# A token-mixing layer on one core: two q and k pairs as plain products, then q, k, xp and four gate tiles as six units of seven block products

## The chip, the cores and the metric

One NeuronCore of one Trainium2 chip. The metric is the device time of one execution in microseconds (us), the median of 3 runs for the kernel before. The profile and the trace are of one further execution of the same program, with a span and a time of its own.

## The reference

```python
# SEQ 1024, D_MODEL 1024, D_FF 2816, POOL_WIDTH 512, 8 heads of 64; depth 1, batch 1, float32
h = x + 0.5 * swiglu(rmsnorm(h, ffn1_norm), ffn1_w_gate_up, ffn1_w_down)
u = rmsnorm(h, mix_norm)
proj = u @ w_in                        # columns: xp 512 | q 512 | k 512 | v 512 | gate logits 2048
y_pool = causal_pool_mixer(xp, pool_w_group, pool_scale) @ w_branch_pool
# four groups of 128 channels: mean over a trailing window of 2, 4, 8, 16 minus the token, then a 128x128 map, a scale
o_sb = stick_breaking_attention(q, k, v)
# per head: z = q.k / 8; A[t,s] = sigmoid(z[t,s]) * prod_{s<j<t} (1 - sigmoid(z[t,j])), s < t; o = A @ v
y_sb = o_sb @ w_branch_attn
g_pool, g_sb = split(sigmoid(gate_logits))
h = h + (g_pool * y_pool + g_sb * y_sb) @ w_out
h = h + 0.5 * swiglu(rmsnorm(h, ffn2_norm), ffn2_w_gate_up, ffn2_w_down)
out = rmsnorm(h, final_norm)
```

## The kernel before

The whole layer is one program with the instructions of each engine written out in their order. TensorE (PE) multiplies, ScalarE (ACT) and VectorE (DVE) prepare operands and take results, GpSimd (POOL) does small work, and SyncE (SP) issues nearly all transfers in one order. Engines meet only through semaphores, and an instruction that waits holds back everything behind it on its engine.

**Products.** Every float32 operand is split in a high part, which ACT copies with rounding (`w_hi`, `u_hi`), and a low part, the rest, which DVE subtracts (`w_lo`, `u_lo`). One product of 128 x 128 by 128 x 512 is then three: high by high, high by low and low by high. One tile of an output projection (128 columns of w_in by 512 tokens, one of PSUM's eight banks) sums over 8 blocks of 128 rows of D_MODEL, so it costs 24 such products. The feed-forward parts and the pool branch save products with a scheme of seven block products in place of eight (`PRODUCTS`: which bank, which sum of weights, and which block or sum of the other side); the projections by w_in are plain.

**Stages.** First feed-forward part 0 to 661.9 us, the front of the mixing block to 883, attention to 1166.5, the attention branch and the out projection to about 1300, second feed-forward part to the end.

**Front** (line 1192 on). `unit_quad` makes two tiles for all tokens in four banks, 96 products, from one unit of weights (`w_raw`, 1 MB, two slots). The order on PE is: two quads for xp, the pooling map of half the groups (`group_quad`, 12 products), values in eight tiles of 24 products in two halves of D_MODEL with the second `group_quad` in between, four units of the pool branch (`pool_branch_unit`, seven products of 6 each), four quads for q and k. Under them ACT copies xp to `xpad`, DVE adds shifted copies of it for the windows (L2327 is a form of it), DVE splits each unit's weights (L1905), q and k are split and stored in `qk_dram`, and the pool branch's result goes to `g_dram`.

**Attention** (line 1383 on). 8 heads of 8 row tiles (`TILE_ORDER` 7, 6, 1, 0, 5, 4, 3, 2; a tile qt has (qt + 1) x 128 columns) give 64 steps and 4 to drain. Each tile goes through a chain over three steps: PE makes the logits (L1334, L1336; in step s); ACT takes the sigmoids `keep` and `a`; GpSimd sets the diagonal to zero (L2626); DVE scans `keep` into the running product (L2471) and multiplies it into `a` (L2475); PE transposes `a` (L1349; in step s + 2); ACT and DVE split what it turned (`at_hi` L1826, `at_lo` L2484); after every second tile PE weighs the values with it (`weigh`, L1365, L1366). The gates' products (L1188) are spread between these as filler: eight units of 96, 768 in all, one unit being gate tile j of the pool branch and gate tile j of the attention branch. `SHARE` says how much of it each step gets, by the row tile:

```python
SHARE = {7: 8, 6: 16, 1: 16, 0: 11, 5: 4, 4: 12, 3: 13, 2: 12}
cut = g0 + (g1 - g0) // 2
gate_parts(g0, cut)
if s >= 4 and s % 2 == 0: weigh((s - 4) // 2)
if 2 <= s < NA + 2: turn(s - 2)
```

Behind the turn come the tile's one or two logits, with the other half of the step's filler after each of them in equal parts. Under attention DVE also splits the gate weights by pieces (L2496), GpSimd multiplies the finished pool gates into y_pool (L2633), and SP loads q and k of a head (L865) two heads ahead; those of heads 0 and 1 are loaded before attention, once the pool branch's result is stored.

## Time and profile before

| | |
|---|---|
| median of 3 runs | 1938.36 us (1938.32 to 1938.59) |
| span of the profiled execution | 1937.1 us |
| that execution's own time | 1938.4 us |
| instructions | 25171 |
| PE busy | 1923.7 us, 99% |
| DVE busy | 1338.3 us, 69% |
| ACT busy | 772.0 us, 40% |
| GpSimd busy | 136.9 us, 7% |
| DMA | 347.20 MB, mean 179 GB/s |

Busy time of PE counts modelled ends of pipelined matmuls, so 99% is not the share in which PE works at its peak. Times in a trace are from the span's start; durations of a group are means.

### The profile page before, as it was taken

The numbers are of one execution on the slowest core, as the hardware profiler recorded it, in microseconds if no ns is written. First come the engines' busy times: TensorE is split into PE (matmuls) and PEld (weight loads), VectorE is DVE, ScalarE is ACT, GpSimd is POOL, SyncE is SP. The second block draws the span as 40 slices with busy tenths as digits, with TensorE's granted clock in tenths as the row PEclk, the third lists the DMA queues.
The fourth block names the chain that finished last, engine by engine and source line by source line (L and its number), as shares of the span: only waits on it lengthen the run. The fifth ranks groups of instructions, "written<-read, shape, count | busy, mean of one in ns | idle before, by whom it ended". The sixth has DMA issues, their size and how long they took to land.

```text
span 1937.1 us, 25171 instructions
## 1 busy us (share of the span) xinstructions
PE 1923.7 (99%) x9094; PEld 1607.4 (83%) x9094; DVE 1338.3 (69%) x1656; ACT 772.0 (40%) x1154; POOL 136.9 (7%) x218
## 2 busy tenths in 40 slices
PE   9999999999999999999999999999999999999998
PEld 9888888888888888888888888888888888888887
DVE  6987777775566667425777778789767776755655
ACT  7423232333434424214565652464323232324344
POOL 1000000000000100002333320010000000000002
PEclk9999999999999999999999999999999999999999
DMA  5456645468676503546645347643535454677665
GB/s 163 148 202 229 226 160 164 171 219 309 201 237 194 179 24 103 177 152 190 164 131 161 108 148 249 206 143 109 183 132 187 149 184 139 221 262 241 206 192 204
DMA packets 245092, 347.20 MB, mean 179 GB/s; under 512 B 16144, under 2 KB 150032, under 8 KB 240400
## 3 DMA queue, kind: packets, MB, share of 16 engines
q1 hardware_dynamic: 245008, 346.09, 54.9%
q8 instruction: 51, 0.84, 0.2%
q14 instruction: 33, 0.27, 0.0%
HBM read 232.79 MB, written 112.98 MB: 178 GB/s over the span
## 4 chain that ended last, share of the span: by engine, by line
PE 55%; DVE 2%; DMA 1%; issue 1%; ACT 1%; SPq 0%; POOL 0%; POOLq 0%; DVEq 0%; ACTq 0%
PE bank L1091 20%; PE bank L1188 12%; PE bank L1135 4%; PE bank L1137 4%; PE bank L1136 4%; PE bank L1047 2%; PE bank L1257 2%; PE bank L1285 2%; PE bank L1349 2%; DMA dn_lo_raw<-act_dram 1%; PE bank L1366 1%; PE bank L1365 1%; PE bank L1336 1%; PE bank L1334 1%; DVE tail_p L2471 0%
## 5 line engine op out<-in xcount | busy, mean ns | idle before, releaser
L1905 DVE TENSOR_TENSOR dn_lo<-dn_lo_raw,dn_hi 128x1024 fp32r<-128x1024 f32 x149 | 181.8, 1224 | 151.6 <-ACT dn_hi L1545 151.2
L1091 PE MATMUL bank<-hi_t,wa_hi 128*128 128x512 f32 x640 | 249.1, 389 | 0.2 <-issue 0.2
L1091 PE MATMUL bank<-hi_t,wa_lo 128*128 128x512 f32 x640 | 249.0, 389 | 0.0
L1091 PE MATMUL bank<-lo_t,wa_hi 128*128 128x512 f32 x640 | 249.0, 389 | 0.0
L1545 ACT ACTIVATE dn_hi<-dn_lo_raw 128x1024 fp32r<-128x1024 f32 x149 | 158.0, 1061 | 217.6 <-DMA dn_lo_raw<-act_dram 217.6
L1135 PE MATMUL bank<-dn_hi 128*128 128x512 f32 x596 | 232.7, 390 | 0.6 <-DVE dn_lo L1905 0.6
L1136 PE MATMUL bank<-dn_hi,dn_lo 128*128 128x512 f32 x596 | 231.9, 389 | 0.0
L1137 PE MATMUL bank<-dn_lo,dn_hi 128*128 128x512 f32 x596 | 231.9, 389 | 0.0
L1091 PE MATMUL bank<-hi_b,wa_hi 128*128 128x512 f32 x480 | 186.9, 389 | 0.5 <-DVE up L2029 0.5
L1091 PE MATMUL bank<-lo_b,wa_hi 128*128 128x512 f32 x480 | 186.8, 389 | 0.0
L1091 PE MATMUL bank<-hi_b,wa_lo 128*128 128x512 f32 x480 | 186.7, 389 | 0.0
L1905 DVE TENSOR_TENSOR wa_lo<-wa_lo_raw,wa_hi 128x1024 fp32r<-128x1024 f32 x132 | 174.3, 1350 | 5.6 <-ACT wa_hi L1485 0.5
L1188 PE MATMUL bank<-u_hi,w_hi 128*128 128x512 f32 x448 | 175.5, 392 | 0.0
L1188 PE MATMUL bank<-u_hi,w_lo 128*128 128x512 f32 x448 | 175.2, 391 | 0.0
L1188 PE MATMUL bank<-u_lo,w_hi 128*128 128x512 f32 x448 | 175.1, 391 | 0.0
L1525 ACT ACTIVATE g<-g 128x512 f32<-128x512 f32 x80 | 50.1, 627 | 263.9 <-DVE g L2037 257.7
L1091 PEld LDWEIGHTS bank<-hi_t,wa_hi 128*128 128x128 f32 x640 | 120.1, 188 | 25.4 <-issue 0.6
L1091 PEld LDWEIGHTS bank<-hi_t,wa_lo 128*128 128x128 f32 x640 | 120.1, 188 | 25.1
L1091 PEld LDWEIGHTS bank<-lo_t,wa_hi 128*128 128x128 f32 x640 | 120.1, 188 | 24.9
L1135 PEld LDWEIGHTS bank<-dn_hi 128*128 128x128 f32 x596 | 111.9, 188 | 24.6 <-DVE dn_lo L1905 1.7
L1137 PEld LDWEIGHTS bank<-dn_lo,dn_hi 128*128 128x128 f32 x596 | 111.9, 188 | 23.3
L1136 PEld LDWEIGHTS bank<-dn_hi,dn_lo 128*128 128x128 f32 x596 | 111.9, 188 | 23.2
(237 smaller groups left out, 3555.3 us busy)
## 6 DMA issues: line engine op xcount, KB each, us to landing
wa_lo_raw<-in_ffn_w_gate_up_dram SPq DMA_DIRECT2D x87, 512.0 KB, 5.0
dn_lo_raw<-act_dram SPq DMA_DIRECT2D x149, 256.0 KB, 4.3
act_dram<-g SPq DMA_DIRECT2D x44, 512.0 KB, 4.5
wd_t<-in_ffn_w_down_dram SPq DMA_DIRECT2D x44, 512.0 KB, 6.6
act_dram<-s_of SPq DMA_DIRECT2D x88, 256.0 KB, 6.5
wd_dram<-wd_t SPq DMA_DIRECT2D x22, 1024.0 KB, 6.0
dn_lo_raw<-wd_dram SPq DMA_DIRECT2D x85, 256.0 KB, 3.3
dn_lo_raw<-in_ffn_w_down_dram SPq DMA_DIRECT2D x64, 256.0 KB, 3.0
```

The source lines that it names most:

```text
L1047: last = nc.tensor.matmul(dst[:, cols], lhs, rhs, start=n == 0, stop=n == 3 * KT - 1, skip_group_check=True)
L1091: last = nc.tensor.matmul(acc, lhs, rhs, start=n == 0 and i != 2 and i < 5, stop=n == 11, skip_group_check=True)
L1135: nc.tensor.matmul(dst, a_hi_[:, toks], w_hi_, start=kf == 0 and DOWN[i][2], stop=False, skip_group_check=True)
L1136: nc.tensor.matmul(dst, a_lo_[:, toks], w_hi_, start=False, stop=False, skip_group_check=True)
L1137: end = nc.tensor.matmul(dst, a_hi_[:, toks], w_lo_, start=False, stop=last, skip_group_check=True)
L1188: last = nc.tensor.matmul(dst, lhs, (rhs_lo if p == 1 else rhs_hi)(kt), start=m == 0, stop=m == 3 * KT - 1)
L1257: last = nc.tensor.matmul(bank[:, b, :], weights(w_lo if p == 2 else w_hi, kt), (rhs_lo if p == 1 else rhs_hi)(kt), start=n == 0, stop=n = ...
L1285: last = nc.tensor.matmul(bank[:, 4 * s + place, :], pool_block(w_lo if p == 2 else w_hi, par, slot)[:, kt, :], rhs, start=n == 0 and i != ...
L1349: last = nc.tensor.transpose(bank[:, 5 + tb % 2, (kb % 4) * P:(kb % 4 + 1) * P], weights_of(n)[:, kb * P:(kb + 1) * P], ident[:, :])
L1525: nc.scalar.activation(g[s][:, half, :], g[s][:, half, :], ACT.Silu).then_inc(silu_ok, 1)
L1545: nc.scalar.activation(hi, raw, ACT.Copy).then_inc(dn_hi_ok, 1)
L1905: return nc.vector.tensor_tensor(dst, raw, hi.bitcast(f32), ALU.subtract)
```

## The change

The matmuls of six projections in the front go to a new unit, `mix_unit`, and two of the eight gate units leave attention.

- q and k of pairs 2 and 3 (heads 0 to 3 in order of time) come first, as two plain quads (`U_A`), right after the first feed-forward part.
- Then six block units (`MIX_UNITS`): q and k of pair 0, of pair 1, the attention branch's gate tiles 0 and 1, then 2 and 3, and the two pairs of xp. Each computes two tiles for 1024 tokens as a 2 x 2 block product with 7 products of 12 in place of 96. ACT and DVE need for it four sums of u (`mix_raw`, `mix_sum`, `tu_*`, 128 x 2048 each; two of the first four raw sums are added by GpSimd), four sums of weights per unit (`ws_*`, 128 x 512 each), and five additions of banks (`mix_c11`, `mix_c22`, `mix_c12`, `mix_c21`). The weights come whole in `ws_raw`, which has one slot: the load of unit b + 1 waits for the last low part of unit b.
- Results of q, k and gates go through a ring of three tiles (`ring_raw`, `ring_hi`, `ring_lo`) to `qk_dram` and `g_dram`; finished gates are read back after attention as those of the other tiles are.
- xp now comes last, so the pooling sums, the pooling map and the values follow in another order: values 0 to 3 of the first half, 0 and 1 of the second, group 0, values 2 and 3, the first half of 4 to 7, group 1, the second half of 4 to 7, then the four units of the pool branch, and attention directly.
- Attention has `NG` = 6 gate units, 576 products. `SHARE` is the same for each row tile; the first step gets 16 shares more (`HEAD_SHARE`). The banks of attention are dealt out anew: gates in 4 and 5, logits in 6, 7 and 0, turned tiles in 1 and 2, outputs in 3.
- Head 0 is loaded after the fourth product of the last branch unit, once the ring's stores have landed; the second slot's load follows behind that unit. ACT's wait for the stored pool branch moves from the start of attention to its third tile.

```diff
+EARLY = 4
+GATE_UNITS = tuple(((0, j), (0, j + 1)) for j in range(0, EARLY, 2)) + tuple(((0, j), (1, j)) for j in range(EARLY, KT))
+NG = len(GATE_UNITS)
+MIX_UNITS = (tuple(("qk", pair) for pair in PAIR_ORDER[2:]) + tuple(("gate", j) for j in range(0, EARLY, 2))
+             + (("xp", 0), ("xp", 1)))
+HEAD_SHARE = 16
 ...
     shares = [SHARE[x["qt"]] for x in TILES] + [4] * DRAIN
+    shares[0] += HEAD_SHARE
     shares[1] += 8
 ...
+            def load_mix(b):
+                kind, which = MIX_UNITS[b]
+                if b:
+                    sp_.wait_ge(mb_lo, 4 * b)
 ...
             def load_head(hn):
 ...
-                    sp_.wait_ge(qk_sp[pair], 32)
+                    sp_.wait_ge(pool_prod, 6 * (KT // 2 - 1) + 4)
+                    for i in range(3):
+                        sp_.wait_ge(ring_sp[i], 32 * ring_uses(i))
 ...
+            def mix_unit(b):
+                s = (b + 1) % 2
+                for i in range(7):
+                    place, hi, lo, (kind, slot) = PRODUCTS[i]
 ...
+                    if i % 2 == 0:
+                        pe.wait_ge(mb_lo, 4 * b + i // 2 + 1)
 ...
+                    if i >= 5:
+                        pe.wait_ge(mb_add, 5 * b + i - 3)
+                    for n in range(12):
+                        kt, p = n // 3, n % 3
+                        if kind == "b":
+                            rhs = u_part(u_lo if p == 1 else u_hi, slot)[:, kt, :]
+                        else:
+                            rhs = (tu_lo if p == 1 else tu_hi)[:, slot, kt, :]
+                        last = nc.tensor.matmul(bank[:, 4 * s + place, :], ws_lo[:, lo, kt, :] if p == 2 else ws_hi[:, hi, kt, :], rhs,
+                                                start=n == 0 and i != 2 and i < 5, stop=n == 11, skip_group_check=True)
+                    last.then_inc(mb_prod, 1)
 ...
-                unit_quad(U_P[m], U_P[m] % 2, Q_P[m], fresh=m == 0)
+                unit_quad(U_A[m], U_A[m] % 2, Q_A[m], fresh=m == 0)
+            for b in range(NM):
+                mix_unit(b)
+            values(0, range(4))
+            values(1, range(2))
             group_quad(0)
-            values(0, range(NT))
-            values(1, range(4))
+            values(1, range(2, 4))
+            values(0, range(4, NT))
             group_quad(1)
             values(1, range(4, NT))
             for u in range(KT // 2):
                 pool_branch_unit(u)
-            for m in range(4):
-                unit_quad(U_QK + m, (U_QK + m) % 2, Q_QK + m)
```

On DVE a block unit is worked off in this order, with parts of the next unit's weights in between:

```diff
+            def mix_unit(b):
 ...
+                mix_c11(b)
+                if b + 1 < NM:
+                    mix_weight_sums(b + 1)
+                    mix_lo(b + 1, 0)
+                mix_out(b, 0, 0, 1)
+                mix_c22(b, 0)
+                if b + 1 < NM:
+                    mix_lo(b + 1, 1)
+                mix_c22(b, 1)
+                mix_out(b, 1, 1, 2)
+                mix_c12(b)
+                if b + 1 < NM:
+                    mix_lo(b + 1, 2)
+                mix_out(b, 0, 1, 3)
```

How the filler changes in a head shows on PE in the second head, from the last logits of row tile 4 to the weighing that stands ahead of the turn of row tile 5. Before:

```order
L1334 MATMUL bank<-k_hi_214,q_st 128x512 [waits sg_ok]
L1336 MATMUL bank<-k_lo_215,q_st 128x512
L1188 MATMUL bank<-u_hi,w_hi 128x512
L1188 MATMUL bank<-u_lo,w_hi 128x512
L1188 MATMUL bank<-u_hi,w_lo 128x512
L1188 MATMUL bank<-u_hi,w_hi 128x512
L1188 MATMUL bank<-u_lo,w_hi 128x512
L1188 MATMUL bank<-u_hi,w_lo 128x512
L1188 MATMUL bank<-u_hi,w_hi 128x512
L1188 MATMUL bank<-u_lo,w_hi 128x512
L1188 MATMUL bank<-u_hi,w_lo 128x512
L1365 MATMUL bank<-at_hi,v_w 128x256 [waits ohi,alo]
```

Of the change:

```order
L1497 MATMUL bank<-k_hi_226,q_st 128x512 [waits sg_ok]
L1499 MATMUL bank<-k_lo_227,q_st 128x512
L1308 MATMUL bank<-u_hi,w_hi 128x512
L1308 MATMUL bank<-u_lo,w_hi 128x512
L1308 MATMUL bank<-u_hi,w_lo 128x512
L1308 MATMUL bank<-u_hi,w_hi 128x512
L1308 MATMUL bank<-u_lo,w_hi 128x512
L1308 MATMUL bank<-u_hi,w_lo 128x512
L1532 MATMUL bank<-at_hi,v_w 128x256 [waits ohi,alo]
```

Nine gate products have become six; the steps around this one shrink alike, and nothing else in a head moves.

On DVE in block unit 0, from its first bank sum to the ones that the sixth product (L2598) and the seventh (L2592) need, the change has (`ws_raw` and `ws_lo` are the weights of unit 1):

```order
L2584 TENSOR_TENSOR ring_raw_208<-bank,ring_raw_208 128x512 [waits mb_prod,mb_copied]
L2567 TENSOR_TENSOR ws_raw<-ws_raw 128x512 [waits mb_in]
L2569 TENSOR_TENSOR ws_raw<-ws_raw 128x512 [waits mb_sum]
L2570 TENSOR_TENSOR ws_raw<-ws_raw 128x512
L2572 TENSOR_TENSOR ws_raw<-ws_raw 128x512 [waits mb_sum]
L2143 TENSOR_TENSOR ws_lo<-ws_raw,ws_hi 128x1024 [waits mb_hi]
L2616 SCALAR_TENSOR_TENSOR ring_lo_211<-ring_raw_208,ring_hi_214 128x512 [waits mb_post]
L2598 TENSOR_TENSOR ring_raw_209<-bank,mid 128x512 [waits mb_prod,mb_copied,ring_sp2]
L2143 TENSOR_TENSOR ws_lo<-ws_raw,ws_hi 128x1024 [waits mb_hi]
L2592 TENSOR_TENSOR ring_raw_209<-bank,ring_raw_209 128x512 [waits mb_add,mb_prod]
```

The first of the four weight sums waits for the weights of unit 1 to land (`mb_in`); the sums of unit 0's own banks, L2598 and L2592, stand behind it.

On SP, where attention's first loads stand, before:

```order
L703 DMA w_raw<-in_w_in_dram 128x8x128 [waits wlo,whi]
L704 DMA w_raw<-in_w_in_dram 128x8x128
L703 DMA w_raw<-in_w_in_dram 128x8x128 [waits wlo,whi]
L704 DMA w_raw<-in_w_in_dram 128x8x128
L816 DMA qk_dram<-qk_hi_207 128x2048 [waits acc_free2,acc_free3,acc_free1,acc_free0]
L816 DMA qk_dram<-qk_lo_209 128x2048
L865 DMA q_st<-qk_dram 64x1024 [waits y_sp3,y_odd_sp,y_sp2,qk_sp2,y_sp1,y_sp0]
L865 DMA q_st<-qk_dram 64x1024
L865 DMA k_hi_214<-qk_dram 64x1024 x2
```

Of the change:

```order
L790 DMA w_raw<-in_w_in_dram 128x8x128 [waits wlo,whi]
L791 DMA w_raw<-in_w_in_dram 128x8x128
L985 DMA q_st<-qk_dram 64x1024 [waits ring_sp1,ring_sp2,ring_sp0,pool_prod]
L985 DMA q_st<-qk_dram 64x1024
L985 DMA k_hi_226<-qk_dram 64x1024 x2
L985 DMA k_lo_227<-qk_dram 64x1024 x2
L944 DMA g_dram<-pst_odd 128x512 [waits acc_free1]
L944 DMA g_dram<-pst 128x512 [waits pool_mid]
L944 DMA g_dram<-pst 128x512 [waits acc_free2]
L944 DMA g_dram<-pst 128x512 [waits acc_free3]
L985 DMA q_st<-qk_dram 64x1024 [waits acc_ready]
```

The first head's load no longer stands behind the stores of q and k in the last quads, and has a wait on the branch's products (`pool_prod`) in place of one on all stores of the pool branch. Those of the last branch unit come behind it.

## Rows read from the trace of the kernel before

**Rows 1.** The page: each engine's busy time, share and instructions; the granted TensorE clock in 40 slices.

```profile
PE 1923.7 (99%) x9094; PEld 1607.4 (83%) x9094; DVE 1338.3 (69%) x1656; ACT 772.0 (40%) x1154; POOL 136.9 (7%) x218
...
PEclk9999999999999999999999999999999999999999
```

**Rows 2.** Timeline of PE in head 2: start us, us, engine, line, operation.

```profile
961.40 0.39 PE L1188 MATMUL bank<-u_hi,w_lo 128*128 128x512 f32 x1
...
963.66 0.40 PE L1188 MATMUL bank<-u_hi,w_hi 128*128 128x512 f32 x1
```

**Rows 3.** Windows: us; PE, PEld, DVE, ACT, POOL busy (x); PEclk, DMA share, GB/s.

```profile
953.54:986.66 33.12, 33.12 (x190) 28.68 (x189) 25.98 (x33) 20.41 (x48) 12.14 (x18) 1.00 0.60 167
707.40:756.40 49.00, 49.00 (x217) 40.42 (x216) 35.82 (x48) 21.81 (x35) 0.00 (x0) 1.00 0.16 49
883.00:1166.50 283.50, 281.26 (x1569) 240.67 (x1568) 218.01 (x264) 167.87 (x388) 97.98 (x144) 1.00 0.52 149
```

**Rows 4.** PE's groups (busy us, mean ns | idle before, releaser) and its table of waits.

```profile
L1349 PE MATMUL bank<-ident,a 128*128 128x128 f32 x288 | 43.1, 276 | 1.0 <-DVE at_lo L2484 0.6 <-DVE a L2475 0.4
...
L1365 PE MATMUL bank<-at_hi,v_w 128*128 128x256 f32 (+1 forms) x160 | 38.2, 274 | 1.2 <-DVE at_lo L2484 1.2
...
PE bank L1285 <- DVE pst L2408: 0.3, 1, 0.3
```

**Rows 5.** Timeline of DVE in one head, 953.54 to 986.66.

```profile
953.54 2.29 DVE L2471 TENSOR_TENSOR_SCAN tail_p<-keep,zero_col 128x1024 f32<-128x1024 f32 x1 [1.05 <-ACT a L1812]
...
965.23 1.16 DVE L2484 TENSOR_TENSOR at_lo<-bank,at_hi 128x512 fp32r<-128x512 f32 x2 [1.76 <-ACT at_hi L1826]
...
973.61 0.96 DVE L2475 TENSOR_TENSOR a<-a,tail_p 128x767 f32<-128x767 f32 x1
...
982.16 0.69 DVE L2475 TENSOR_TENSOR a<-a,tail_p 128x511 f32<-128x511 f32 x1
982.77 0.78 DVE L2496 TENSOR_TENSOR w_lo<-w_raw,w_hi 128x512 fp32r<-128x512 f32 x1
```

**Rows 6.** Timeline of PE in the same head.

```profile
966.49 0.34 PE L1365 MATMUL bank<-at_hi,v_w 128*128 128x256 f32 x1
...
974.87 0.84 PE L1349 MATMUL bank<-ident,a 128*128 128x128 f32 x6
...
983.35 0.62 PE L1349 MATMUL bank<-ident,a 128*128 128x128 f32 x4
```

**Rows 7.** Groups of DVE; then DMA issues: KB each, us to landing.

```profile
L1996 DVE TENSOR_TENSOR wa_lo_raw<-wa_lo_raw 128x512 f32<-128x512 f32 x40 | 27.7, 692 | 1.4
...
L2327 DVE TENSOR_TENSOR s_a<-xpad 128x1039 f32<-128x1039 f32 x4 | 5.0, 1240 | 11.3 <-ACT xpad L1700 7.4 <-issue 3.7
...
L1905 DVE TENSOR_TENSOR w_lo<-w_raw,w_hi 128x2048 fp32r<-128x2048 f32 x13 | 29.8, 2291 | 10.7 <-ACT w_hi L1658 10.7
...
w_raw<-in_w_in_dram SPq DMA_DIRECT2D x32, 512.0 KB, 5.9
...
k_lo<-qk_dram SPq DMA_DIRECT2D x16, 256.0 KB, 6.3
```

**Rows 8.** GpSimd's multiply as a group and in the timeline, with DVE's scans of 384.

```profile
L2633 POOL TENSOR_TENSOR gst<-gst,pool_y 128x512 f32<-128x512 f32 x16 | 21.3, 1333 | 19.1 <-ACT gst L1854 19.1
...
982.98 1.72 POOL L2633 TENSOR_TENSOR gst<-gst,pool_y 128x512 f32<-128x512 f32 x1
...
983.47 2.04 DVE L2471 TENSOR_TENSOR_SCAN tail_p<-keep,zero_col 128x384 f32<-128x384 f32 x1
...
1150.69 0.96 DVE L2471 TENSOR_TENSOR_SCAN tail_p<-keep,zero_col 128x384 f32<-128x384 f32 x1 [0.24 <-POOL a L2626]
```

**Rows 9.** Timeline: PE and DVE at the first branch unit, SP at the head's load.

```profile
756.56 0.39 PE L1285 MATMUL bank<-yp_hi,w_hi 128*128 128x512 f32 x1
...
759.65 0.41 DVE L2285 TENSOR_TENSOR v_st<-bank,v_st 128x256 fp32r<-128x256 f32 x1
...
871.48 1.24 SPq L865 DMA_DIRECT2D k_lo<-qk_dram  x2
```

More of the change, by code:

```diff
@@ L443, in macaron_layer @@
         ms_sum = sem("ms_sum")
-        late_in = [sem(f"late_in{i}") for i in range(3)]
         part_ok = sem("part_ok")
@@ L1681, in take_qk @@
-            def take_qk(m):
-                for b in range(4):
-                    th, ab = b // 2, b % 2
-                    if b == 0 and m >= 2:
-                        act.wait_ge(qk_sp[m - 2], 32)
-                    act.wait_ge(acc_ready, 4 * (Q_QK + m) + b + 1)
-                    c = ab * SEQ + th * HALF
-                    nc.scalar.activation(qk_hi[m % 2][:, c:c + HALF], bank[:, b, :], ACT.Copy,
-                                         scale=1.0 if ab else QSCALE).then_inc(ev_hi, 1)
@@ new lines, in mix_sums_hi, with mix_hi @@
+            def mix_sums_hi(slot, sums):
+                act.wait_ge(rt_sum, sums)
+                nc.scalar.activation(tu_hi[:, slot], tu_raw[:, slot], ACT.Copy).then_inc(rt_hi, 1)
+            def mix_hi(b, g):
+                if g in (0, 3):
+                    act.wait_ge(mb_in, 32 * (b + 1))
+                else:
+                    act.wait_ge(mb_sum, 4 * b + 2 * g)
+                mix_free(act, b, g)
+                nc.scalar.activation(ws_hi[:, mix_group_hi(g)], ws_raw[:, mix_group(g)], ACT.Copy).then_inc(mb_hi, 1)
@@ new lines, in mix_post @@
+            def mix_post(b, a, th, adds):
+                kind = MIX_UNITS[b][0]
+                if kind == "xp":
+                    return
+                act.wait_ge(mb_add, 5 * b + adds)
+                if kind == "gate":
+                    nc.scalar.activation(mix_dst(b, a, th), mix_dst(b, a, th), ACT.Sigmoid).then_inc(mb_post, 1)
+                else:
+                    nc.scalar.activation(ring_hi[tile_of(b, a) % 3][:, th * HALF:(th + 1) * HALF], mix_dst(b, a, th), ACT.Copy,
+                                         scale=1.0 if a else QSCALE).then_inc(mb_post, 1)
@@ new lines, in mix_weight_sums @@
+            def mix_weight_sums(b):
+                a11, a12, s2, s1, s3, s4, a21, a22 = (ws_raw[:, s].rearrange("p k f -> p (k f)") for s in range(8))
+                dve.wait_ge(mb_in, 32 * (b + 1))
+                nc.vector.tensor_tensor(s1, a21, a22, ALU.add).then_inc(mb_sum, 1)
+                dve.wait_ge(mb_sum, 4 * b + 1)
+                nc.vector.tensor_tensor(s2, s1, a11, ALU.subtract).then_inc(mb_sum, 1)
+                nc.vector.tensor_tensor(s3, a11, a21, ALU.subtract).then_inc(mb_sum, 1)
+                dve.wait_ge(mb_sum, 4 * b + 2)
+                nc.vector.tensor_tensor(s4, a12, s2, ALU.subtract).then_inc(mb_sum, 1)
@@ new lines, in mix_lo, with mix_c11 @@
+            def mix_lo(b, g):
+                dve.wait_ge(mb_hi, 4 * b + g + 1)
+                low(flat(ws_lo[:, mix_group(g)]), flat(ws_raw[:, mix_group(g)]), flat(ws_hi[:, mix_group_hi(g)])).then_inc(mb_lo, 1)
+            def mix_c11(b):
+                dve.wait_ge(mb_copied, 2 * b + 1)
+                dve.wait_ge(mb_prod, 7 * b + 2)
+                dst = mix_dst(b, 0, 0)
+                nc.vector.tensor_tensor(dst, bank[:, 4 * ((b + 1) % 2) + 1, :], dst, ALU.add).then_inc(mb_add, 1)
@@ L2613, in _, with mix_raw @@
             norm_rows(1)
+            def mix_raw(slot):
+                nc.gpsimd.tensor_tensor(tu_raw[:, slot], u_part(u_hi, slot).bitcast(f32), u_part(u_lo, slot).bitcast(f32), ALU.add).then_inc(ut_raw, 1)
             pool.wait_ge(dn_ok, TAKEN)
-            nc.gpsimd.memset(xpad[:, :, 0:PAD], 0.0).then_inc(const_set, 1)
+            pool.wait_ge(tr_free, 3 * NT)
+            mix_raw(1)
+            for t in (6, 7):
+                pool.wait_ge(h_sp[t], 16)
+            pool.wait_ge(xn_ok, 2 * NT)
+            mix_raw(0)
+            for m in range(2):
+                pads_free(pool, m)
+                nc.gpsimd.memset(xpad[m][:, :, 0:PAD], 0.0).then_inc(const_set, 1)
             def weights_of(n):
```

685 lines of the change are left out of this document (448 added, 237 removed).

## The prediction

> **What bounds the kernel now.** I read the page first: TensorE (PE) is busy for 99% of a span of 1937.1 us, at a granted clock of full speed, 2.4 GHz, in all 40 slices [rows 1]. The reader should see that no other engine comes near, and then distrust the 99%, since matmuls overlap in the records. The timeline gives the price that counts: one 128x512 product is recorded as 0.39 us long, but eleven of them start 2.26 us apart from first to last [rows 2], which is 0.226 us each (0.2267 over longer runs). That is the unit of every sum below. The windows by stage come next [rows 3]: the front, from the first projection to attention, 661.9 to 883 us, has a single wait of 0.3 us [rows 4]; attention, 883 to 1166.5, has 218 us of VectorE (DVE) work in 283.5. The table of PE's waits lists about 2 us for attention (L1349 and L1365), with slacks so thin that they decide this case.
>
> **Products saved.** Before, the two xp pairs and four q/k pairs cost 6 x 96 products and the eight gate pairs 768. Now two pairs stay plain (192), six units cost 7 x 12 = 84 each (504), and six gate units remain (576). 1344 become 1272: 72 fewer, 72 x 0.2267 = **16.3 us**. By place, the front gains 120 products (+27.2 us) and attention loses 192 (-43.5 us). The kernel is as long as PE if PE is never starved, so the question is what those 192 hid.
>
> **Attention.** The gate products are filler. A tile's logits go out in step s; ScalarE (ACT), GpSimd's mask, DVE's scan and multiply follow; PE turns the result in step s+2. I compare the end of the multiply with the start of the transposes over one head [rows 5, 6]: for qt 5, 974.57 against 974.87 (slack 0.3 us); for qt 3, 982.85 against 983.35 (0.5); and at_lo of qt 6 ends at 966.39 with PE's weighing at 966.49 (0.1). The other turns have about a microsecond or more. SHARE is unchanged, so each head's filler falls from 87.6 to 63.1 products, by 28%. Between logits and turn of a tile lie a quarter (half for one-chunk tiles) of its own step's filler, all of the next and half of the one after. For qt 5 that is about 1 + 11.5 + 6 products, of which 5.2 go: 1.2 us against 0.3 of slack, so PE waits 0.9. For qt 3, 6 + 11.5 + 4 lose 6: 1.4 against 0.5, wait 0.9. For the weighing after qt 6, half of steps 0 and 5 lose 2: 0.5 against 0.1, wait 0.4. The other turns lose about as much as they have, and the waits ahead of them cover the rest. Sum 2.2 us a head. A second reading agrees: from this scan of qt 7 to the next the head takes 33.1 us, and DVE is busy for 26.0 of them [rows 3, 5]. It is idle for 7.1, of which 24.5 products, 5.6 us, would go: DVE would have to be busy for 94% of the time, in short chains that each wait for ACT and PE. The first head gets extra filler (HEAD_SHARE), so 7 x 2.2 = **15.4 us** of waits. From below it could be nothing, if DVE starts earlier as PE hurries; from above some 24 us, if each of the eight turns waits for DVE's own queue.
>
> **Front: six block units.** No row shows this form here, so I take the ordinary 128x512 product [rows 2] at 0.2267; a unit is 19.0 us. DVE does per unit five bank sums and four weight sums of 128x512 (0.69 us each), three low parts of 128x1024 at 1.23 and, for q and k, four more of 0.69 [rows 7]: 12 to 13 us, which fits. The order does not fit everywhere. The next weights can be loaded only when the last low part of this unit is done, and DVE then stands before the weight sums while c22, which the sixth product needs at 5 x 2.72 = 13.6 us, is behind them. In unit 0 the last low part is at about 4 us (DVE takes the last plain bank first); 5.9 us to landing plus the spilled megabytes ahead of it [rows 7] gives 10.5, then four sums, a low part, an output and the add, 4.7 us (5.4 by durations, less some 0.09 by which neighbours overlap, as 982.16 + 0.69 does with 982.77 [rows 5]): 15.2 against 13.6, 1.6 us late. Units 1 and 2 start the load at 1.5 and come out at 12 to 14: I take 0.4 to 0.5 each. Together **2.5 us** (between 0 and 8: if each of five loads lands 1.5 us later than this, every unit waits). The sums of u before unit 0 are hidden: DVE has 8 bank takes, 2 raw sums, 4 sums, 4 low parts of 128x2048 at 2.29 and 6.4 us for weights, 35 us in all, under 43.5 us of plain products. GpSimd's two sums of 128x2048 have no row; its 128x512 multiply is 1.33 us [rows 8], so between 1.3 and 5.3 each, and I take 5.3: done at about 676, wanted at 679 by DVE's third step.
>
> A rule speaks against exactly these two. While GpSimd's multiply ran from 982.98 to 984.70, the scan of 384 columns took 2.04 us, where it takes 0.96 at 1150.69 [rows 8]. The Trainium skill, "SBUF — State Buffer", "Who interferes with whom", says that a DVE instruction with two inputs in SBUF and a GpSimd instruction that reads SBUF block one another for the whole instruction. By that rule a 5.3 us sum started at 664 holds back the scaling of the last row tile; without the rule the sum would have no term for it. It has none here either, since the tile's transposes come only at 671.
>
> **Front: values, pooling, branch.** xp comes last now, so its windows are summed after the block units and not under plain products. From the last block product PE has 216 products to the first branch product, 49.0 us, the same stretch as 707.4 to 756.4 [rows 3]. DVE must do there: four pool tiles (ten shifted adds, four finishing and four low parts, all 1.23: 21 us with the overlap), two full weight splits (4.4), the value tiles (8 x 0.7), group takes (6), sums and low parts of y (11.5), weight sums (3), small ones (1.3) and about 3 us waiting for ACT in between: 56. Before, it was through at 760.06, 3.5 us after the branch began at 756.56, and PE waited 0.3 for L2408 [rows 4, 9]. Now 7 us after: PE waits **3.4 us** more (1 to 6). The first value product waits for the split that ends behind the last block unit, **0.4**.
>
> **Attention's start.** The four q/k units that lay here are gone. SP may load head 0 only after the fourth of seven products of the last branch unit. Two issues take 1.24 us [rows 9], so the sixth starts 3.1 us after the first, and it lands 5.9 to 6.3 us later [rows 7]: about 9.2 us. PE has 18 products (4.1 us) and eight of filler (1.8) until the first logits, so **3.3 us** (0 to 5; SP issues a megabyte of gate weights just ahead). ACT's table load moves to an earlier place and costs nothing: it sits in idle time of ACT under the first plain bank.
>
> **After attention** the banks of branch and gates swap; the out projection's first wait moves one step later: a gain under 0.3 us, taken as 0.
>
> **Sum** for the profiled execution, span 1937.1 and 1.3 us around it, which I take at the median 1938.4: -16.3 + 15.4 + 2.5 + 3.4 + 0.4 + 3.3 = +8.7, so **1947 us**.
>
> **Rivals.**
> (A) The forecast: attention runs short of filler and the front of cover. 0.50, 1936 to 1962.
> (B) Faster. DVE and ACT are fed as much earlier as PE is, so that the chains shrink with the steps and waits in attention stay at 3 us; the front loses 4. For it: DVE still has 7.1 us idle in a head [rows 3]. Against it: the idle stands where DVE waits for ACT to copy what PE turned (1.76 us before at_lo at 965.23 [rows 5]), so it shrinks only as far as PE turns earlier, and PE turns late. It decides if the waits stay under 5 us in attention; with 5 in the whole kernel it would be 1927. 1938.4 - 16.3 + 7 = 1929. Chance 0.26, counting mixtures under 1934.5.
> (C) Waits of 8 us in attention and 8 in the front: no change, 1938. Chance 0.19 with its surroundings.
> (D) The block stage falls behind for good: raw weights land at 13 us of each unit instead of 8, because two q/k megabytes are spilled ahead, and GpSimd's two long sums hold DVE. Six units late by 3 us are 18 instead of 2.5: 1962. Chance 0.05.
> (E) The change doesn't do what it says (products not fewer): PE's count of rows falls by 72, 5975 to 5903, so no chance.
>
> **How the numbers follow.** A measurement of this kernel can tell a difference of about 0.2%, 3.9 us: faster is below 1934.5, slower above 1942.2. The range takes (A) with its unknown bounds, most of (B) down to 1927, and stops at 1961: attention 24 and front 15 would be 1938.4 - 16.3 + 39 = 1961. Faster 0.26; same 0.20 (C, and the low edge of A); slower 0.54.
>
> **What would show it.** PE in attention waiting for DVE a and at_lo some 17 us in all, most at the transposes of qt 5 and qt 3; the stage about 256 us plus the start, not 240. A wait of 2 to 4 us before the first logits on the q_st load. A wait of 3 to 4 us in the first branch unit for pst. In the block units DVE standing on the ws_raw load, PE waiting 1 to 2 us at the sixth product of unit 0. Wrong if PE's waits over the whole kernel stay under 10 us, or if most of them lie in the front.

## Result and profile after

The changed kernel takes 1958.05 us (median of 4 runs, 1955.97 to 1959.06) against 1938.34 us: slower by 19.7 us, ratio 1.0100 with a 95% interval of 1.0086 to 1.0114. The forecast was 1947.0. The profiled execution, the longest of the four, has a span of 1957.0 us against 1937.1, and the table below accounts for these 19.9 us.

The page of the changed kernel:

```profile
span 1957.0 us, 25185 instructions
...
PE 1919.6 (98%) x9022; PEld 1596.1 (82%) x9022; DVE 1409.4 (72%) x1732; ACT 792.4 (40%) x1174; POOL 150.2 (8%) x221
...
PEclk9999999999999999999999999999999999999999
```

PE has 72 matmuls fewer (9094 to 9022), as announced, and is busy for only 4.1 us less: a slow clock came in, and the first 0.16 us of every new wait counts as busy, as shown below. A slice of 49 us is too coarse to show either, so the table of waits is next (line of PE, what it waited for: us in total, times, longest us):

```profile
PE bank L1532 <- DVE at_lo L2849: 7.8, 12, 1.5
PE bank L1514 <- DVE a L2840: 5.0, 10, 0.7
PE bank L1514 <- DVE at_lo L2849: 4.0, 7, 0.9
PE bank L1497 <- DMA k_lo<-qk_dram: 3.8, 1, 3.8
PE bank L1447 <- DVE ring_raw L2598: 2.6, 2, 1.7
PE bank L1413 <- DVE pst L2739: 1.8, 1, 1.8
...
PE bank L1413 <- ACT pst L1970: 1.8, 1, 1.8
```

The first three are attention (weighing and turns), where [rows 4] had 1.0 and 1.2 us. Then come the first head's load, block units 0 and 1, and the first branch unit. Every wait that the prediction listed outside attention is there, and attention has 16.8 us in all where it had 15.4 on top of some 2. **But these are recorded idle times, and they are too small.** A product is recorded as 0.39 us long while the next starts after 0.227 [rows 2], so the record of the last one before a wait covers the wait's first 0.16 us, and a wait shorter than that leaves no note. At the largest wait of a head, in the timeline of PE:

```profile
1055.43 0.39 PE L1308 MATMUL bank<-u_hi,w_hi 128*128 128x512 f32 x1
1055.65 0.39 PE L1308 MATMUL bank<-u_lo,w_hi 128*128 128x512 f32 x1
1057.52 0.39 PE L1532 MATMUL bank<-at_hi,v_w 128*128 128x256 f32 x1 [1.48 <-DVE at_lo L2849]
```

From start to start it is 1057.52 - 1055.65 = 1.87 us, less 0.227 is 1.64 lost, noted as 1.48. I count all waits in this way, start to start against the usual step of that form, and call it "by starts". Turns and weighings then lose 24.6 us, against 3.5 before. Such a sum runs over 96 places and the usual step is known to about 0.01 us, so a total may be off by some 0.5 us.

Stages by windows (us, busy times of PE, PEld, DVE, ACT, POOL, clock, DMA share, GB/s); the front now ends at 917.5, attention at 1188.0:

```profile
661.90:917.50 255.60, 249.05 (x1099) 203.69 (x1097) 182.58 (x212) 94.04 (x126) 10.21 (x6) 1.00 0.36 117
917.50:1188.00 270.50, 248.84 (x1378) 206.37 (x1377) 213.16 (x256) 157.80 (x369) 104.31 (x144) 0.99 0.52 145
...
920.00:924.00 4.00, 0.71 (x2) 0.62 (x3) 0.00 (x0) 0.00 (x0) 0.00 (x0) 0.80 1.02 326
924.00:928.00 4.00, 4.00 (x11) 3.14 (x10) 0.00 (x0) 1.98 (x4) 0.54 (x2) 0.50 1.06 287
928.00:932.00 4.00, 4.00 (x17) 3.24 (x16) 3.22 (x3) 1.44 (x4) 0.00 (x0) 0.85 1.02 243
...
922.40:929.20 6.80, 5.91 (x14) 4.67 (x15) 0.46 (x1) 2.69 (x5) 0.54 (x2) 0.50 1.06 308
```

The last four rows are what nothing in the forecast had: PE stands still for 3.8 us before the first logits, and the granted clock is at the lower level, 1.2 GHz, from 922.4 to 929.2 us, as the last row shows; the 0.80 and 0.85 are means over both levels. Eleven products start in 4 us where there are 17 or 18 at 2.4 GHz. In the timeline of PE they stand 0.43 us apart:

```profile
919.11 0.39 PE L1308 MATMUL bank<-u_lo,w_hi 128*128 128x512 f32 x1
923.29 0.80 PE L1497 MATMUL bank<-k_hi,q_st 128*128 128x512 f32 x1 [3.79 <-DMA k_lo<-qk_dram]
923.88 0.63 PE L1499 MATMUL bank<-k_lo,q_st 128*128 128x512 f32 x1
924.31 0.63 PE L1308 MATMUL bank<-u_hi,w_lo 128*128 128x512 f32 x1
924.73 0.63 PE L1308 MATMUL bank<-u_hi,w_hi 128*128 128x512 f32 x1
```

| part | forecast, us | in the trace, by starts, us |
|---|---|---|
| 72 products fewer | -16.3 | -16.3 |
| turns and weighings in attention | +15.4 | 24.6 - 3.5 = +21.1 |
| head 0's load | +3.3 | +4.0 |
| block units 0 and 1 | +2.5 | 1.9 + 1.1 = +3.0 |
| first branch unit | +3.4 | 1.95 + 2.0 - 0.46 = +3.5 |
| first value product | +0.4 | +0.5 |
| slow clock | 0 | +2.8 (12 steps of 0.43 and two of 0.59 and 0.34 in place of 0.227) |
| sum | +8.7 | +18.6 of 19.9 |

So of the missing 11 us, 5.7 are in attention and 2.8 in the clock of this execution. The 1.3 us that the sum lacks are a net of two things that the stages show: attention is 2.6 us longer than these terms make it, and the stages behind it are 1.6 us shorter (770.6 us before, 769.0 after), where three waits of 0.3 to 0.7 us of the kernel before, at 1211, 1753 and 1920 us, are gone. The experiments ask whether the filler is the cause in attention, how its waits hang together, and what the clock costs.

### The profile page after: what moved, and what is told of

Its sections match the earlier page's. It is cut to its first block, busy times and chain, and to the rows that moved or that the text cites. A ratio compares the mean times of both kernels' runs of the same rounds, so it can differ in the third digit from the quotient of the medians.

```text
span 1957.0 us, 25185 instructions
## 1 busy us (share of the span) xinstructions
PE 1919.6 (98%) x9022; PEld 1596.1 (82%) x9022; DVE 1409.4 (72%) x1732; ACT 792.4 (40%) x1174; POOL 150.2 (8%) x221
## 4 chain that ended last, share of the span: by engine, by line
PE 86%; DVE 8%; ACT 2%; DMA 2%; issue 1%; POOL 0%; SPq 0%; POOLq 0%; ACTq 0%; DVEq 0%
PE bank L1211 39%; PE bank L1255 8%; PE bank L1256 8%; PE bank L1257 8%; PE bank L1308 5%; PE bank L1167 4%; PE bank L1447 4%; DVE tail_p L2836 3%; PE bank L1384 2%; PE bank L1356 2%; PE bank L1413 2%; DVE a L2840 1%; PE bank L1514 1%; DVE at_lo L2849 1%; PE bank L1142 1%
## 5 line engine op out<-in xcount | busy, mean ns | idle before, releaser
L1211 PEld LDWEIGHTS bank<-lo_t,wa_hi 128*128 128x128 f32 x640 | 120.1, 188 | 24.9
L2962 POOL TENSOR_SCALAR mean_eps<-mean_sq 128x1 f32<-128x1 f32 x28 | 11.1, 396 | 1374.1 <-ACT u_lo_raw L1592 622.6
L1211 PEld LDWEIGHTS bank<-hi_b,wa_hi 128*128 128x128 f32 x480 | 90.1, 188 | 19.5 <-DVE up L2267 0.9
L1211 PEld LDWEIGHTS bank<-hi_b,wa_lo 128*128 128x128 f32 x480 | 90.1, 188 | 18.8
```

What stands on the lines that cost most here:

```text
L1211: last = nc.tensor.matmul(acc, lhs, rhs, start=n == 0 and i != 2 and i < 5, stop=n == 11, skip_group_check=True)
```

## Experiments

In all of them the kernel before ran beside on the same chip, with medians of 1937.98 to 1938.30 us, so their times can be set beside the 1958.05 us of the changed kernel. Its own four executions spread over 3.1 us, though: a median that differs from 1958.05 by 1 to 2 us does not decide anything, and there the waits and the clock in the traces must.

**1. Filler put back** (`dup`), one run.

```diff
+                    if m % 3 == 2:
+                        nc.tensor.matmul(bank[:, 4 + fb % 2, :], w_lo[:, j % 2, ab, m // 3, :], u_hi[:, m // 3, cols],
+                                         start=False, stop=False)
                     last = products(bank[:, 4 + fb % 2, :], j % 2, ab, lambda kt: u_hi[:, kt, cols],
```

> The changed kernel, with every third gate product in attention (u_hi by w_lo) issued twice, so that attention has 768 filler products again as before the change; the doubled low term is all that differs in what is computed. Theory 1 (attention waits because it has too little filler): +192 products are +43.5 us, and the recorded idle of PE before transposes and weighing falls from 16.8 us to 2 to 4 us, with some 0.16 us more per wait that the overlap of the records hides: 1958 + 43.5 - 20 = 1981 us (1977 to 1985). Theory 2 (the new banks or the new order cost it, not the number): waits stay, 2001 us.

1977.9 us, with

```profile
PE bank L1517 <- DVE a L2843: 0.7, 1, 0.7
PE bank L1517 <- DVE at_lo L2852: 0.7, 3, 0.2
...
PE bank L1535 <- DVE at_lo L2852: 0.3, 1, 0.3
```

for turns and weighings: 1.7 us in place of 16.8, or by starts 3.3 in place of 24.6. 43.5 us of work cost 19.8, so 23.7 came back, of which 21.3 are these waits. Theory 1.

**2. Filler taken from the kernel before** (`thin`), one run.

```diff
+                    if m % 4 == 2:
+                        continue
                     last = products(bank[:, fb % 2, :], j % 2, ab, lambda kt: u_hi[:, kt, cols],
```

> The kernel before, with every fourth gate product in attention left out (so the gates lack part of their sum): 576 filler products instead of 768, with the old banks, the old front and the old loads. Theory 1: saves 43.5 us of products and brings 17 to 21 us of waits for a and at_lo: 1938.3 - 43.5 + 19 = 1914 us (1910 to 1918). Theory 2: no new waits, 1895 us.

1921.6 us. The gate products of every fourth place are left out, so 576 remain. The waits of the old attention with the new amount of filler:

```profile
PE bank L1367 <- DVE at_lo L2486: 6.9, 10, 2.6
PE bank L1351 <- DVE at_lo L2486: 5.4, 6, 1.8
PE bank L1351 <- DVE a L2477: 5.0, 11, 1.3
```

By starts 24.4 us, the changed kernel's 24.6, with the old banks, loads and order: the amount of filler alone makes them. The time is 7.6 us above the 1914 of theory 1 and outside its range. Behind two of its waits (2.0 us at 896.6, 2.75 at 1016.5) the clock was at the lower level for 3.4 us each (897.4 to 900.8 and 1016.9 to 1020.3), which is 3.4 us lost in all; with 20.9 us of new waits by starts that leaves some 2.5, which I did not trace.

**3. The head's wait filled** (`busy`).

```diff
+                if c == 0:
+                    for i in range(18):
+                        nc.tensor.matmul(bank[:, 6, :], w_hi[:, 0, 0, i % KT, :], u_hi[:, i % KT, 0:HALF], start=True, stop=True,
+                                         skip_group_check=True)
                 if n % NT == 0 and part == 0:
                     pe.wait_ge(head_in[slot], 96 * (x_["head"] // 2 + 1))
```

The wait for the logits' bank moves ahead of these products.

> The changed kernel, with 18 products (4.1 us) without a use put on PE just ahead of its wait for head 0's load, into the bank of the first logits. They fill the wait of 3.8 us, so the logits start at the same time or 0.3 us later. Theory 1 (the granted clock fell to half from about 923 us on because PE stood still there): the clock stays at 1.00 and products behind it are 0.227 us apart at once, not 0.43: 1958 - 3.5 = 1954.5 us. Theory 2 (the clock fell for another reason, such as the crowded DMA queues): the dip to 0.5 stays, 1958 us.

Median 1956.8 us (1955.5 to 1957.4); the profiled execution has a span of 1953.5 against 1957.0. The same stretches:

```profile
920.00:924.00 4.00, 4.00 (x19) 3.30 (x19) 0.00 (x0) 0.07 (x1) 0.00 (x0) 1.00 1.03 332
924.00:928.00 4.00, 4.00 (x20) 3.34 (x19) 1.14 (x2) 2.62 (x5) 0.54 (x2) 1.00 1.06 271
```

The DMA share is as high as before and the clock stays full, so it is PE's standing still that counts. In this pair of executions 3.5 us went, but it sets the longest of one kernel's four executions against the shortest of the other's; between the medians it is 1.3, less than expected and within the spread. Theory 1 in kind, its price left open for run 16.

**4. No gates in the front** (`early0`).

```diff
-EARLY = 4
+EARLY = 0
```

> The changed kernel with EARLY = 0: no gate tiles in the front, so four block units (q and k of pairs 0 and 1, xp) and eight gate units, 768 filler products. Against the changed kernel: attention +192 products, front -168: +24 products, +5.4 us; waits in attention -18 to -21 us; the head load's wait and the slow clock behind it (7.5 us) stay, as do the branch's two waits (4 us). Theory 1: 1958 + 5.4 - 19 = 1944 us (1940 to 1948). Theory 2 (waits come from what else is new in attention): 1963 us.

1947.6 us (1946.9 to 1948.4), ratio 1.0046 (1.0029 to 1.0063). Waits at turns and weighings are 4.0 us by starts, so another 20.6 came back. A new one appears, which I had not foreseen, since the first xp unit now follows the last q and k unit and shares two slots of the ring with it:

```profile
PE bank L1447 <- ACT xpad L1865: 7.1, 1, 7.1
```

**5. Head 0 loaded first** (`sporder`).

```diff
             spill_pool_branch(2)
-            gate_unit(1)
 ...
             load_head(0)
+            gate_unit(1)
             spill_pool_branch(3)
```

> The changed kernel, with SP loading head 0 ahead of the second gate unit's megabyte instead of behind it. The load cannot start earlier (it waits for the fourth product of the last branch unit), but it has less of the DMA engines' time to share. Theory 1 (the wait at the first logits is transfer time): it lands 1 to 2 us sooner, the wait falls from 3.8 to about 2.3 us, and the slow clock behind it gets shorter or goes: 1955 us (1953 to 1957). Theory 2 (the wait is issue and latency): nothing, 1958 us.

1960.4 us (1958.9 to 1961.5). The wait is 3.5 us instead of 3.8: theory 2. From the first issue of the load to the first logits it is 9.35 us instead of 9.65, so the megabyte ahead of it cost 0.3. In the profiled execution the clock also fell behind the waits at 723 and 887 us (by starts 2.02 and 2.01), to the lower level for 3.4 us each, which it had not done in that of the changed kernel behind 1.88 and 2.00 us; the median is 2.3 us above that kernel's.

**6. Another spread** (`share`).

```diff
-SHARE = {7: 8, 6: 16, 1: 16, 0: 11, 5: 4, 4: 12, 3: 13, 2: 12}
+SHARE = {7: 7, 6: 17, 1: 15, 0: 11, 5: 0, 4: 13, 3: 13, 2: 16}
```

> The changed kernel with another SHARE, {7: 7, 6: 17, 1: 15, 0: 11, 5: 0, 4: 13, 3: 13, 2: 16}: same 576 products, less of them in the step of row tile 5 and more in that of row tile 2. Theory 1 (the shortage is of the whole head: DVE's chains and PE's turns need some 30 us): a better spread takes 3 to 6 of the 24 us of waits in attention away, most stay: 1953 us (1951 to 1956). Theory 2 (the waits come from a spread that no longer fits): they fall to below 8 us, 1941 us.

1955.4 us (1953.6 to 1957.3); 21.2 us of waits by starts, 3.4 less. Theory 1: another spread takes a small part, and the range given for it (1951 to 1956) holds.

**7. The ring's slots moved** (`e0ring`).

```diff
+def ring_slot(n):
+    return n % 3 if n < FIRST_TILE or EARLY else (n + 1) % 3
```

The ring's stores, waits and counts use this slot in place of `n % 3`; `EARLY` is 0.

> EARLY = 0 again, with the last two tiles of the ring in other slots (1 and 2 in place of 0 and 1), so that the first xp unit need not wait for the store of the last k tile. In the run with EARLY = 0 PE waited 7.1 us there (7.3 by starts), with a slow clock behind it. Theory 1: that wait goes, and 1 to 3 us of slow clock with it: 1947.6 - 9 = 1938.5 us (1936 to 1941). Theory 2 (the wait moves to the next unit, for the last tile's store): 1943 to 1947 us.

1940.8 us (1939.4 to 1942.7), ratio 1.0014 (1.0004 to 1.0023). The wait of 7.1 us is down to 0.8.

**8. First logits behind all of step 0's filler, and SP's order of run 5** (`e0best`), on top of run 7, with HEAD_SHARE 20.

```diff
-                cut = g0 + (g1 - g0) // 2
+                cut = g1 if s == 0 else g0 + (g1 - g0) // 2
```

> The same with all of step 0's filler (25 products, HEAD_SHARE 20) put ahead of the first logits and head 0 loaded ahead of the second gate unit. 14 more products than before stand in front of the wait, 3.2 us, and the load lands 1 us sooner, so the wait of 2.8 us and its slow clock go: another 3 to 5 us: 1934.5 us (1932 to 1938), faster than both kernels. Rival: the later first logits push waits into the next steps, and DVE and ACT work of the first head begins as late as before: 1938 us.

1945.3 us (1943.5 to 1947.4): worse than run 7. The head's wait is gone, but

```profile
PE bank L1519 <- DVE at_lo L2854: 7.3, 3, 5.7
```

shows 5.7 us at one turn, that of tile 6 in the first head (904.71 us), with 6.8 us at the lower clock around it. The rival, and stronger.

**9. c22 first** (`c22`), in DVE's block unit.

```diff
                 mix_c11(b)
-                if b + 1 < NM:
-                    mix_weight_sums(b + 1)
-                    mix_lo(b + 1, 0)
                 mix_out(b, 0, 0, 1)
                 mix_c22(b, 0)
                 if b + 1 < NM:
-                    mix_lo(b + 1, 1)
+                    mix_weight_sums(b + 1)
+                    mix_lo(b + 1, 0)
                 mix_c22(b, 1)
+                if b + 1 < NM:
+                    mix_lo(b + 1, 1)
```

> The changed kernel, with DVE's order in a block unit altered: the first c22 sum stands ahead of the next unit's four weight sums, not behind them. Theory 1 (PE waits for c22 because DVE stands on the weights' load): the two waits of 1.9 and 1.1 us by starts in units 0 and 1 go, the next unit's weights are still split in time (11.6 + 8 us against 19.0): 1958 - 3 = 1955 us (1953 to 1957, less where a slow clock behind the first wait goes too). Theory 2 (the weights are then late and the wait moves to the next unit's start): 1958 us or more.

1958.9 us (1958.8 to 1960.5). Unit 0's wait only fell from 1.9 to 1.5 us by starts, and stands at the next product now, whose sum (L2592) now stands behind the weight sums:

```profile
PE bank L1447 <- DVE ring_raw L2592: 2.8, 3, 1.3
```

The time is as in theory 2, the place as in neither: the waits stay inside the units. Both bank sums come while DVE has the next weights to do.

**10. Two sums to GpSimd** (`gps`).

```diff
-                    nc.vector.tensor_tensor(dst, yp_hi[:, 2:4, cols].bitcast(f32), yp_lo[:, 0:2, cols].bitcast(f32),
-                                            ALU.add).then_inc(rt_raw, 1)
 ...
+                nc.gpsimd.tensor_tensor(yt_raw[:, slot], yp_hi[:, 2:4, cols].bitcast(f32), yp_lo[:, 0:2, cols].bitcast(f32),
+                                        ALU.add).then_inc(rt_raw, 1)
```

> The changed kernel, with the two 128x1024 sums of yp_hi and yp_lo ahead of the branch (2.4 us of DVE, where DVE is busy without a pause from 823 to 882 us) given to the idle GpSimd, at 2.3 us each going by its 4.6 us for 128x2048. Theory 1 (GpSimd and a DVE instruction with two inputs in SBUF keep one another out, as DVE's scaling of 5.61 us beside GpSimd's sum shows): DVE is held for some 4.6 us in place of 2.4, and the two branch waits grow by 2 us: 1960 us (1958 to 1962). Theory 2 (they run side by side): DVE is through 2.4 us earlier, 1955.6 us.

1959.4 us (1958.4 to 1960.2). The sums took 4.75 us on GpSimd, and DVE, which needs them at once, stood for 4.95 us. That says nothing on whether the two exclude one another, because DVE had nothing to run beside them. What it shows is that this work is on DVE's path: the first wait in the branch grew from 1.94 to 2.62 us, so nothing was won by handing it to a slower engine.

**11. DVE's weight splits cut** (`cut`).

```diff
+                kts = slice(kts.start, kts.start + 1)
                 last = nc.vector.tensor_tensor(flat(w_lo[:, par, ab, kts, :]), flat(w_raw[:, par, ab, kts, :]),
```

> The changed kernel, with DVE's 20 splits of gate weights under attention (L2861) cut from 128x512 to 128x128, so that most of the low parts of five gate units are not computed and the gates miss part of their sum. Takes 20 x 0.40 = 8 us of work from DVE in attention and nothing from PE. Theory 1 (DVE's whole load bounds the heads): the waits in attention, 24 us by starts, fall by 6 to 8: 1951 us. Theory 2 (the chain of one tile through ACT, GpSimd, DVE and PE is too long for the filler that is left, with DVE's queue only in part): they fall by 1 to 3: 1956 us.

1956.3 us (1954.3 to 1956.6), 22.1 us of waits by starts: 2.5 less for 8 us of work. Theory 2, by the waits; the medians are too close.

**12. Runs 8 and 9 on top of 7, SP's order as it was** (`e0fix`).

> EARLY = 0 with the ring's last slots moved, all of step 0's filler (25 products) ahead of the first logits, and the c22 order of the run above; SP's order as in the changed kernel. Against EARLY = 0 with the ring moved (1940.8 us): the head's wait of 2.7 us goes with its slow clock (1 to 2), the units' waits of 2.8 us go: 1940.8 - 7 = 1934 us (1931 to 1937), faster than both kernels. Rival: with the first logits 3 us later the stores of the pool branch or ACT hold the first head back as in the run with SP's other order, 1938 us.

1941.9 us (1939.5 to 1943.8), not faster than run 7. The head's wait of 2.8 us by starts went, and 2.7 us came at the turn of tile 6 (902.11 us, for at_lo): a later first logit makes the whole first chain later. The order of run 9 brought nothing here either: the waits in the block units are 4.4 us by starts against 3.8. The same turn waited for 5.8 us in run 8, so the other 3 us there came with SP's order, the one difference between the two in this place; through which wait, no run shows.

**13, 14. DVE's order in attention** (`turn7`, `turn13`).

```diff
-                turned_first = 2 <= s <= NA and TILES[s - 1]["qt"] in (1, 5, 3)
+                turned_first = 2 <= s <= NA and TILES[s - 1]["qt"] in (7, 1, 5, 3)
```

and `in (1, 3)` for the second.

> The changed kernel; under attention DVE takes the low part of the turned tile ahead of the next tile's scan in four steps of eight (next tile 7, 1, 5 or 3) in place of three (1, 5 or 3). The largest wait of a head, 1.6 us by starts at the weighing ahead of the turn of tile 7, is for such a low part behind the scan and multiply of 3.5 us for tile 7. Theory 1 (each wait is its own lack of cover): the 1.6 us goes and little comes for it: 1958 - 7 x 1.4 = 1948 us. Theory 2 (DVE's queue is one chain in which the scans of tile 7 and 6 are late as well): the wait moves to the turns of 7 and 6 and grows: 1958 to 1963 us.

> The same with two steps (next tile 1 or 3): the scan of tile 5 stands ahead of the low part of the tile turned before. Theory 1: PE waits longer for that low part, 1958 to 1962 us. Theory 2 (what counts is that the long scans 5 and 4 start early, since their turns wait in every head): the 0.7 and 0.4 us of waits at the turns of 5 and 4 shrink: 1954.5 us (1953 to 1957).

1965.0 us (1963.3 to 1966.5) and 1954.9 us (1954.5 to 1956.3). By starts, in sums over the eight heads:

| wait at | before | changed | turn7 | turn13 |
|---|---|---|---|---|
| weighing ahead of turn 7, and the last one | 1.6 | 8.0 | 0.7 | 8.0 |
| turn 7 | 0 | 0 | 5.2 | 0 |
| turn 6 | 1.0 | 2.6 | 10.5 | 2.9 |
| weighing ahead of turn 1 (of tiles 7 and 6) | 0 | 2.9 | 2.2 | 2.9 |
| weighing ahead of turn 5 | 0 | 0 | 0 | 4.7 |
| turn 5 | 0.3 | 5.4 | 5.4 | 0 |
| turn 4 | 0.3 | 3.0 | 3.0 | 0.7 |
| turn 3 | 0 | 2.1 | 2.1 | 2.1 |
| turn 2 | 0.4 | 0.9 | 0.9 | 0.9 |
| all | 3.6 | 24.9 | 30.0 | 22.2 |

Theory 2 in both. The 7 us that go at one place come back as 13 at the next two. In the changed kernel, DVE around that largest wait:

```profile
1053.45 2.28 DVE L2836 TENSOR_TENSOR_SCAN tail_p<-keep,zero_col 128x1024 f32<-128x1024 f32 x1
1055.77 1.22 DVE L2840 TENSOR_TENSOR a<-a,tail_p 128x1023 f32<-128x1023 f32 x1
1056.91 0.55 DVE L2849 TENSOR_TENSOR at_lo<-bank,at_hi 128x384 fp32r<-128x384 f32 x1
1057.38 2.01 DVE L2836 TENSOR_TENSOR_SCAN tail_p<-keep,zero_col 128x896 f32<-128x896 f32 x1
```

PE's weighing starts at 1057.52, as soon as the 0.55 us are done. They stand behind the 3.5 us for tile 7, and if they go first, as in turn7, the scans of 7 and 6 and with them the turns of 7 and 6 are late. The four instructions shown run without a pause, and so does the multiply behind them, while over the head (1031.00 to 1062.00 us) DVE is busy for only 25.5 of 31 us.

**15, 16. All long waits filled** (`allbusy`, `e0busy`).

```diff
+                    if u == 0 and i in (2, 5):
+                        wait_bank(0, Q_B)
+                        fill(8, 0)
 ...
+                    if b == 0 and i == 5:
+                        wait_bank(0, Q_A[1] + 1)
+                        fill(8, 0)
```

The first logits have the products of run 3 ahead of them. Run 16 has the same on the kernel of run 7, with 12 ahead of the first logits.

> The changed kernel with products without a use in front of the four longest waits: 8 before the sixth product of block unit 0, 8 before the third and 8 before the sixth of the first branch unit, 18 before the first logits. Each group takes about as long as the wait it stands in, so nothing starts later by over 0.3 us. Theory 1 (waits of 1.7 us and more let the granted clock fall for some microseconds, not at every one and not in every execution): no stretch below full clock in the front or in attention, 1955.5 us (1954 to 1957), with a narrower spread. Theory 2 (the clock falls for other reasons, and the fill costs its overlaps): 1957 to 1959 us.

> EARLY = 0 with the ring's last slots moved (1940.8 us), with the same products without a use (12 before the first logits). Theory 1: 1940.8 - 2.5 = 1938.3 us (1937 to 1940), level with the kernel before. Theory 2: 1940 to 1942 us.

1957.0 us (1956.6 to 1958.4) and 1938.3 us (1937.6 to 1939.7, ratio 1.0001, 0.9992 to 1.0010). In both profiled executions no stretch of the front or of attention is below full clock. The second took 2.5 us off run 7, as expected, from products that compute nothing. The first took only 1.0 off the changed kernel, between the theories and within the spread. So the slow clock cost 2.5 us of a median where it can be told (run 16 against run 7, with 11 and 10 executions), and in the changed kernel 1.0 to 1.3, which its spread does not let one tell; the 2.8 are those of one execution.

No version that computes everything beat the kernel before; run 16 equals it. (Run 2 is shorter because it leaves out a quarter of the gate products.)

## Why the prediction was right and wrong

**Right**: the direction, the mechanism, and the place of every wait outside attention. The kernel is as long as PE, 72 products are 16.3 us, and both experiments on the filler alone (1 and 2, one execution each) show that the 192 products taken from attention hid some 20 us of chains. The head's load (4.0 by starts against 3.3, with the terms of its sum: start at the fourth product, six issues, landing), the block units (3.0 against 2.5), the branch unit (3.5 against 3.4) and the value split (0.5 against 0.4) came out as worked out. In the stretch from 823 to 882 us DVE was busy for 55.9 of 59 us, which is the "56" of that step. Rival (B) wanted under 5 us of waits in attention; there are 24.6, so the chains did not shrink with the steps, and even 8 us less work for DVE gave only 2.5. Rival (C) wanted 8 us there. Rival (D) wanted 3 us in each of six block units; only units 0 and 1 wait for over half a microsecond, 3.0 us in all.

**Wrong, first step**: "Sum 2.2 us a head", from turns 5 and 3 and the weighing behind tile 6, 15.4 us in all. By starts attention lost 21.1, which is 3.0 in each of seven heads. The three places that the sum names gave only 10: turn 5 5.4 where 6.3 was forecast, the weighing behind tile 6 2.9 where 2.8 was, and turn 3 2.1 in place of 6.3. That the total came as near as it did is in part luck, for the other 11 us are at places to which the prediction gave nothing, with the sentence "The other turns lose about as much as they have, and the waits ahead of them cover the rest": the weighing ahead of turn 7, 6.4 us more than before and the largest of all, turn 4 with 2.7, turn 6 with 1.6 and turn 2 with 0.5. The sign that the prediction named, most of the waits at turns 5 and 3, did not show: they have 7.5 of 24.9 us.

The slack of that weighing could have been read from the trace of before. Just behind the head of [rows 5] DVE ends the low part that it needs at 990.68, 1.1 us ahead of it:

```profile
990.13 0.55 DVE L2484 TENSOR_TENSOR at_lo<-bank,at_hi 128x384 fp32r<-128x384 f32 x1
...
991.80 0.28 PE L1365 MATMUL bank<-at_hi,v_w 128*128 128x256 f32 x1
```

The weighing of tiles 3 and 2 stands there in seven heads. The slack was 0.9 to 1.4 us at five of them and nothing at two: at 1025.97 PE waited 1.06 us already, and at 1093.15 0.05. In the changed kernel PE waits there each time, for 0.5 to 1.6 us. I had compared cover and chain for single turns of one head and taken the waits ahead as help; in DVE's order a late scan makes the low parts and scans behind it late as well. The mechanism was right and the term mis-sized by 5.7 us.

**Wrong, second step**: no term for the clock. The profile of before is at full clock in every slice and PE's waits there are short [rows 1, 4]; a kernel that was forecast to stand for 3.3 us at one place, and 2 at others, leaves the stretch for which that row speaks. The profiled execution lost 2.8 us to it; in the median it is less, as runs 3, 15 and 16 say.

**What else held**: GpSimd's long sum beside DVE. It took 4.6 us (5.3 was taken), and DVE's scaling of the last row tile, which takes 1.28 us otherwise, took nearly as long as both together:

```profile
664.17 5.61 DVE L2150 SCALAR_TENSOR_TENSOR u_lo_raw<-h,rstd,gain 128x1024 f32<-128x1024 f32 x1 [0.98 <-POOL rstd L2967]
```

```profile
664.10 4.59 POOL L2982 TENSOR_TENSOR tu_lo_raw<-u_hi,u_lo 128x2048 f32<-128x2048 f32 x1
```

The Trainium skill, "SBUF — State Buffer", "Who interferes with whom", has such a pair block one another for the whole instruction, and this trace agrees: DVE's instruction, which began 0.07 us after GpSimd's, became 4.3 us longer. It cost nothing, for the reason given, as the tile's transposes came at 671.08.

What stays open: which steps inside attention make its other 2.6 us, and why three waits behind it are gone; in run 2, some 2.5 us; what the clock cost in the median of the changed kernel; why the clock falls behind one wait of 2 us and not behind the same wait in another execution; and whether GpSimd and DVE would have held one another up in run 10, which its dependency hid.

## What to carry to other kernels

Work that fills another engine's gaps is worth its own time only once, when it is removed, less all that it hid: here 192 products of 43.5 us gave back 22. Before taking filler out of a pipelined stage, list the slack of every wait in the period, those at its border too, in several periods and not in one, and add up along the queue that serves them; a wait that is not zero before has no slack at all.

Read waits from start to start when records overlap, and expect a slow clock at a new stop of PE of 2 us at times, and at one of 3 us each time (counts below): moving a load or a filler does not help if the chain behind starts later, but products without a use in the gap keep the clock up.

## What the runs showed of the hardware

- The granted clock fell to the lower level, 0.50, for 3.4 or 6.8 us at a time, beginning between 2.8 us before the end of a stop of PE and 1.3 us after it. In the 18 profiled executions, up to PE's last product, it did so at each of the 15 stops of 2.7 us and more (by starts), at 11 of the 40 of 1.8 to 2.6 us, and at none of the 30 of 1.3 to 1.7. With useless products in the stops it stayed at 1.00 (runs 3, 15, 16).
- A DVE instruction with two inputs in SBUF was stretched from 1.28 to 5.61 us by a GpSimd sum of 4.59 us that had begun 0.07 us before. GpSimd's next sum, 4.61 us from 669.94 on, ran beside four DVE instructions with one input in PSUM and one in SBUF (`u_lo<-bank,u_hi`), which took 2.47 us together; in the kernel before, where GpSimd has no such sum, the same four took 2.48.
- Recorded idle time of PE behind a 128x512 product is 0.16 us less than the time lost (1.48 against 1.64).
